# The last 32 tokens' gate of a hybrid decoder step: computed in four column groups, its embedding product in another bank, its x and p loaded ahead of time

## What is computed

```python
    x = x + mixed @ w_out
    xn2 = _rmsnorm(x, norm_ffn_g)
    x = x + _peer(xn2.reshape(B * L, D_MODEL), peer_wq, peer_keys, peer_u, peer_v).reshape(B, L, D_MODEL)
    gate = jax.nn.sigmoid(_rmsnorm(x, norm_pl_g) @ w_pl_gate)
    x = x + gate * (p @ w_pl)
    ...
    y_sample = _rmsnorm(hs, final_norm_g)
```

## Time and profile before

| | us |
|---|---|
| median of 3 runs | 3205.69 (3203.79 to 3205.81) |
| the profiled execution | 3209.12 |
| its span in the trace | 3207.1 |
| mean granted TensorE clock | 0.856 of 2.4 GHz |
| PE busy | 2387.9 (74%) |
| DVE busy | 2238.4 (70%) |
| POOL busy | 1325.4 (41%) |
| ACT busy | 951.4 (30%) |

### The profile page before, as it was taken

One profiled execution on the slowest core, in us unless ns is written; L12 is line 12 of the kernel. 1 busy time (PEld: TensorE's weight loads), 2 busy tenths in 40 slices (PEclk: granted clock), 3 DMA queues, 4 the chain that ended last, 5 costly groups with the idle time before them and its releaser, 6 DMA issues.

```text
span 3207.1 us, 53243 instructions
## 1 busy us (share of the span) xinstructions
PE 2387.9 (74%) x20836; PEld 951.4 (30%) x20836; DVE 2238.4 (70%) x5463; ACT 951.4 (30%) x2428; POOL 1325.4 (41%) x1143
## 2 busy tenths in 40 slices
PE   8879999567877778757876767576678676767666
PEld 3643333223333333213432222122222221212112
DVE  1366667768878788756667667587777777777764
ACT  2212232325335344212322222132323232232222
POOL 0024444324334344435565544344444444444441
PEclk9989999888888889867788878788888887888877
DMA  6579999999999999999999999999999999999994
GB/s 262 184 289 421 421 412 419 417 417 390 418 392 406 416 417 416 413 409 418 417 415 412 416 417 394 418 411 420 408 414 407 420 419 421 404 419 407 421 420 183
DMA packets 202995, 1266.96 MB, mean 395 GB/s; under 512 B 24144, under 2 KB 27496, under 8 KB 61040
## 3 DMA queue, kind: packets, MB, share of 16 engines
q0 software_dynamic: 159808, 1133.76, 86.1%
q1 hardware_dynamic: 41500, 129.51, 10.2%
q10 hardware_dynamic: 1436, 0.29, 0.0%
HBM read 1235.00 MB, written 28.65 MB: 394 GB/s over the span
## 4 chain that ended last, share of the span: by engine, by line
DMA 30%; PE 15%; DVE 6%; POOL 3%; issue 3%; ACT 2%; DVEq 2%; POOLq 0%; ACTq 0%
DMA ring<-in_uv,idx 30%; PE sc L964 7%; DVE ring L1793 3%; PE sc L997 3%; POOL ring L1975 3%; PE route L939 1%; DVEq L1803 1%; PE sc L966 1%; ACT diag L1334 1%; PE work L985 0%; POOL front L1991 0%; ACT hgelu L1329 0%; PE sc L863 0%; PE sc L661 0%; PE sc L957 0%
## 5 line engine op out<-in xcount | busy, mean ns | idle before, releaser
L1975 POOL DMA_INDIRECT ring<-in_uv,idx x1056 | 1246.9, 1181 | 1655.0 <-PE sc L966 1417.6
L1793 DVE CUSTOM_DVE_ANT_0 ring<-ring,xn_cur 128x1024 f32<-128x1024 f32 x1056 | 1280.6, 1222 | 651.0 <-DMA ring<-in_uv,idx 646.4
L964 PE MATMUL sc<-ring,diag 32*32 32x512 f32 x8192 | 1240.8, 725 | 656.2 <-ACT diag L1334 607.9
L966 PE MATMUL sc<-ring,diag 32*32 32x512 f32 x8192 | 1240.9, 725 | 0.0
L964 PEld LDWEIGHTS sc<-ring,diag 32*32 32x32 f32 x8192 | 271.3, 118 | 1437.9 <-ACT diag L1334 1037.1
L1329 ACT ACTIVATE hgelu<-hdot 128x2 f32<-128x2 f32 x528 | 107.5, 204 | 1821.5 <-DVE hdot L1793 1820.5
L1334 ACT ACTIVATE diag<-gate_d,hgelu 128x32 f32<-128x32 f32 x1056 | 281.8, 314 | 21.2
L966 PEld LDWEIGHTS sc<-ring,diag 32*32 32x32 f32 x8192 | 270.6, 118 | 2.3 <-issue 2.3
L521 PE MATMUL sc<-big,front 128*128 128x512 f32 x448 | 209.0, 611 | 4.6 <-DVE front L1439 4.6
L1329 ACT ACT_TABLE_LOAD x128 | 164.2, 1283 | 2.3
L939 PE MATMUL route<-big,xnT 128*128 128x256 f32 x560 | 138.8, 403 | 0.0
(11 more groups left out here) (271 smaller groups left out, 2340.8 us busy)
## 6 DMA issues: line engine op xcount, KB each, us to landing
front<-wqk_scratch SPq DMA_DIRECT2D x27, 1024.0 KB, 13.1
ring<-in_uv,idx POOLq DMA_INDIRECT x1056
big<-in_w_in SPq DMA_DIRECT2D x8, 1024.0 KB, 14.4
wqk_scratch<-front SPq DMA_DIRECT2D x8, 1024.0 KB, 6.6
big<-wqk_scratch SPq DMA_DIRECT2D x8, 1024.0 KB, 22.5
x<-x_scratch SPq DMA_DIRECT2D x13, 512.0 KB, 8.8
front<-in_x SPq DMA_DIRECT2D x8, 512.0 KB, 8.1
xnT<-in_wq_t POOLq DMA_DIRECT2D x8, 512.0 KB, 4.8
```

The lines of the kernel that those rows point to most:

```text
L964: pe.matmul(sc[own, 0, :], diag[own, r, :], uv_rows[own, r, D:D + W4], start=opens_sum, stop=closes).then_inc(row_added[r], 1)
L966: pe.matmul(sc[other, 1, :], diag[own, r, :], uv_rows[own, r, D + W4:2 * D], start=opens_sum, stop=closes).then_inc(row_added[r], 1)
L1793: dve.tensor_tensor_reduce(uv_rows[:, k % RING, 0:D], uv_rows[:, k % RING, 0:D], xn_cur[:, :], 1.0, 0.0, ALU.mult, ALU.add, hdot[:, n % 2, ...
L1975: pool.indirect_dma_start(uv_rows[:, k % RING, :], None, uv, bass.IndirectOffsetOnAxis(ap=idx[:, n % PH, j:j + 1], axis=0)).then_inc(row_i ...
```

## The change

Jobs 0 to 7, the prompt tiles, stay as they are, except that tile 8 leaves `GATE_JOBS`. Tile 8's gate gets functions of its own:

- **x.** SP loads the 32 rows into `xn_next` (`x2_s`) at s = 514, as soon as DVE has copied `xn_next` for tile 8, and no longer into `x2` after tile 7's y is stored.
- **p.** SP loads it at s = 525, after PE's last embedding matmul of tile 7, and no longer after tile 7's y.
- **Embedding.** PE computes it right behind the last `add_rows`, before it waits for x, for all 1024 columns at once: column group q (partitions 32q to 32q+31 of bank RT) holds columns 256q to 256q+255.
- **Gate.** x is turned in 32-row blocks (8 transposes to 128 x 32 in one bank), scaled by one DVE instruction, and multiplied by w_gate in four column groups in bank S0, 32 matmuls of 256 columns.
- **Sigmoid.** One activation of 128 x 256, with the norm factor copied to all four groups by three small DVE copies.
- **The end.** Four DVE products of 32 x 256 bring the groups back to 32 x 1024; then one addition, squares, root, reciprocal, scaling and the store, on 32 partitions.

```diff
-GATE_JOBS = [(4, 322), (0, 342), (3, 361), (5, 384), (1, 404), (6, 448), (2, 468), (7, 512), (8, NN * PAIRS)]
+GATE_JOBS = [(4, 322), (0, 342), (3, 361), (5, 384), (1, 404), (6, 448), (2, 468), (7, 512)]
...
+        x2_s = xn_next[0:NS, :]
+        junk_s = xn_cur[0:NS, :]
+        prod_s = xnT[0:NS, :, :].rearrange("p a b -> p (a b)")
+        x2T_s = cut(fr, 8192, KD, NS)
+        sig_s = cut(fr, 8448, D // QUADS)
...
+            def sample_gate():
+
+                pe.wait_ge(p_in, 16 * (NT + 1))
+                pe.wait_ge(free[RT], opens(RT, "sample embed", QUADS))
+                for k in range(2):
+                    for q in range(QUADS):
+                        mm = pe.matmul(bank[RT][group[q], 0:D // QUADS], p_sb[:, k, 0:NS], wpl[:, k, quarter[q]],
+                                       start=(k == 0), stop=(k == 1))
+                        if k == 1:
+                            mm.then_inc(ready[RT], 1)
+                pe.wait_ge(x2_ready, 2 * (NT + 1))
+                pe.wait_ge(free[TA], opens(TA, "sample x2"))
+                for k in range(KD):
+                    mm = pe.transpose(bank[TA][:, k * NS:(k + 1) * NS], x2_s[:, k * T:(k + 1) * T], ident[0:NS, 0:NS])
+                mm.then_inc(ready[TA], 1)
+                pe.wait_ge(free[S0], opens(S0, "sample gate", QUADS))
+                pe.wait_ge(free[TA], emptied(TA, "sample x2"))
+                for k in range(KD):
+                    for q in range(QUADS):
+                        mm = pe.matmul(bank[S0][group[q], 0:D // QUADS], x2T_s[:, k, :], wg_sb[:, k, quarter[q]],
+                                       start=(k == 0), stop=(k == KD - 1))
+                        if k == KD - 1:
+                            mm.then_inc(ready[S0], 1)
...
-            for step in range(13):
-                gate_step(len(GATE_JOBS) - 1, step)
+            sample_gate()
...
+            act.wait_ge(x2_sq, NT + 1)
+            act.activation(gst[0:NS, RT2:RT2 + 1], gst[0:NS, NS2:NS2 + 1], ACT.Sqrt).then_inc(x2_root, 1)
+            act.wait_ge(r2_ready, NT + 1)
+            act.wait_ge(ready[S0], filled(S0, "sample gate"))
+            act.activation(sig_s, bank[S0][:, 0:D // QUADS], ACT.Sigmoid, scale=gst[:, R2:R2 + 1]).then_inc(free[S0], 1)
+            act.wait_ge(y_sq, NT + 1)
+            act.activation(gst[0:NS, RT3:RT3 + 1], gst[0:NS, NS3:NS3 + 1], ACT.Sqrt).then_inc(y_root, 1)
...
+            def sample_gate():
+
+                dve.wait_ge(x2_s_in, 16)
+                for r in range(RING):
+                    dve.wait_ge(row_added[r], added(NN * TOPK))
+                dve.tensor_tensor(x2_s[:, 0:W4], x2_s[:, 0:W4], sc[0:NS, 0, :], ALU.add).then_inc(x2_ready, 1)
+                dve.tensor_tensor(x2_s[:, W4:D], x2_s[:, W4:D], sc[NS:2 * NS, 1, :], ALU.add).then_inc(x2_ready, 1)
+                dve.drain()
+                dve.tensor_tensor_reduce(junk_s, x2_s, x2_s, 1.0, 0.0, ALU.mult, ALU.add, gst[0:NS, NS2:NS2 + 1])
...
+                for q in range(QUADS):
+                    ins = dve.tensor_tensor(prod_s[:, quarter[q]], sig_s[group[q], :], bank[RT][group[q], 0:D // QUADS],
+                                            ALU.mult)
+                ins.then_inc(free[RT], 1)
+                dve.drain()
+                dve.tensor_tensor(x2_s, x2_s, prod_s, ALU.add)
...
-                if t == NT:
-                    sp.dma_start(y_s, x2[0:NS, :]).then_inc(y_out, 16)
+                sp.dma_start(y_p[tile_rows(t), :], x2[:, :]).then_inc(y_out, 16)
+                if t == NT - 1:
                     return
...
+                if s == N0 * PAIRS + 2:
+                    sp.wait_ge(xn_moved, NT + 1)
+                    sp.dma_start(x2_s, x1_d[SEQ:SEQ + NS, :]).then_inc(x2_s_in, 16)
+                if s == GATE_JOBS[-1][1] + 13:
+                    sp.wait_ge(ready[WK], filled(WK, ("embed", len(GATE_JOBS) - 1, 1)))
+                    load_p(NT)
```

More of the change, by code:

```diff
@@ L341, in front_and_experts @@
         g_pl = cut(fr, 12544, KD)
+        x2_s = xn_next[0:NS, :]
[3 more added lines that the diff above has]
+        sig_s = cut(fr, 8448, D // QUADS)
+        group = [slice(q * NS, (q + 1) * NS) for q in range(QUADS)]
+        quarter = [slice(q * D // QUADS, (q + 1) * D // QUADS) for q in range(QUADS)]
         sc = whole.enter_context(nc.psum_tensor("sc", [T, 4, 512], f32))
@@ L435, in front_and_experts @@
         x2_in = sem("x2_in")
+        x2_s_in = sem("x2_s_in")
         p_in = sem("p_in")
@@ L1836, in add_sum @@
                 dve.wait_ge(x2_in, 16 * X2_LOADS[t])
-                end = NN if t == NT else (t + 1) * PH
                 for r in range(RING):
[L1839 to L1843, removed]
+                    dve.wait_ge(row_added[r], added((t + 1) * PH * TOPK))
+                dve.tensor_tensor(x2[:, 0:W4], x2[:, 0:W4], sc[:, 0, :], ALU.add).then_inc(x2_ready, 1)
+                for m in range(QUADS):
                     own, other = slice(m * NS, (m + 1) * NS), slice((m ^ 1) * NS, ((m ^ 1) + 1) * NS)
@@ L1887, in gate_step @@
                                              in1=g_fin, op0=ALU.mult, op1=ALU.mult).then_inc(y_ready, 1)
+            def sample_gate():
[6 more added lines that the diff above has]
+                dve.tensor_tensor_reduce(junk_s, x2_s, x2_s, 1.0, 0.0, ALU.mult, ALU.add, gst[0:NS, NS2:NS2 + 1])
+                mean_eps(gst[0:NS, NS2:NS2 + 1], D).then_inc(x2_sq, 1)
+                dve.wait_ge(ready[TA], filled(TA, "sample x2"))
+                dve.tensor_tensor(x2T_s, bank[TA][:, 0:KD * NS].rearrange("p (a b) -> p a b", a=KD),
+                                  g_pl.unsqueeze(2).to_broadcast([T, KD, NS]), ALU.mult).then_inc(free[TA], 1)
+                dve.wait_ge(x2_root, NT + 1)
+                dve.reciprocal(gst[0:NS, R2:R2 + 1], gst[0:NS, RT2:RT2 + 1])
+                dve.drain()
+                for q in range(1, QUADS):
+                    dve.tensor_copy(gst[group[q], R2:R2 + 1], gst[0:NS, R2:R2 + 1])
+                dve.drain()
+                dve.sem_inc(r2_ready, 1)
+                dve.wait_ge(free[S0], emptied(S0, "sample gate"))
+                dve.wait_ge(ready[RT], filled(RT, "sample embed"))
+                for q in range(QUADS):
+                    ins = dve.tensor_tensor(prod_s[:, quarter[q]], sig_s[group[q], :], bank[RT][group[q], 0:D // QUADS],
+                                            ALU.mult)
+                ins.then_inc(free[RT], 1)
+                dve.drain()
+                dve.tensor_tensor(x2_s, x2_s, prod_s, ALU.add)
+                dve.drain()
+                dve.tensor_tensor_reduce(junk_s, x2_s, x2_s, 1.0, 0.0, ALU.mult, ALU.add, gst[0:NS, NS3:NS3 + 1])
+                mean_eps(gst[0:NS, NS3:NS3 + 1], D).then_inc(y_sq, 1)
+                dve.wait_ge(y_root, NT + 1)
+                dve.reciprocal(gst[0:NS, R3:R3 + 1], gst[0:NS, RT3:RT3 + 1])
+                dve.drain()
+                dve.scalar_tensor_tensor(out=x2_s, in0=x2_s, scalar=gst[0:NS, R3:R3 + 1], in1=g_fin[0:NS, :],
+                                         op0=ALU.mult, op1=ALU.mult).then_inc(y_ready, 1)
@@ L1944, in _ @@
                         gate_step(i, s - s0)
-            add_sum(NT)
-            for step in range(16):
-                gate_step(len(GATE_JOBS) - 1, step)
+            sample_gate()
         @block.gpsimd
@@ L2245, in step @@
                 for i, (t, s0) in enumerate(GATE_JOBS):
-                    if t < NT and s == s0 + 16:
+                    if s == s0 + 16:
                         after_gate(i)
+                if s == N0 * PAIRS + 2:
[4 more added lines that the diff above has]
+                    load_p(NT)
             load_x(0)
@@ L2268, in _ @@
                 step(s)
-            after_gate(len(GATE_JOBS) - 1)
+            sp.wait_ge(y_ready, NT + 1)
+            sp.dma_start(y_s, x2_s).then_inc(y_out, 16)
             sp.wait_ge(y_out, 16 * (NT + 1))
```

3 lines of the change are left out of this document (removed).

## The result

The changed kernel takes 3188.09 us (median of 5 runs, 3185.96 to 3192.11), the kernel before beside it 3205.81 (5 runs, 3203.79 to 3207.86): ratio 0.9941, 95% interval 0.9930 to 0.9951. On another chip, later, it took 3186.26 (4 runs) against 3207.24, ratio 0.9938 (0.9922 to 0.9953). The forecast was 3185.0 with a range of 3180 to 3191: faster, as forecast, and inside the range; 17.7 us of the 20.7 forecast show in the medians. The profiled execution of the changed kernel, 3185.96 us with a span of 3184.0, is the fastest of its five, and that of before was 3.4 us above its median, so the 23.1 us between the spans flatter the change. What can be compared is the tail: from the end of PE's last row sum to the end of the span. It was 39.2 us and is 19.6. The other 3.5 of the 23.1 lie before it, where the loop has hardly been changed.

The account below looks back on a forecast made before the run. Bound: the serial chain at the end, after the expert fetches. Savings of 3.3 us from x, about 14.8 to the gate's end and 3.2 after, less 0.6 for loads, give 20.7: 3205.69 - 20.7 = 3185.0 us, range 3180 to 3191.

Parts of the forecast that it names:

- The bound of x: Before tile 8's first addition: loading x early gives 3.3 us and no more, up to PE's last row sum.
- Embedding and transposes: On PE between row sums and gate: hidden beside DVE's sum and squares, counted as nothing; worst end costs 0.4 us.
- The gate's matmuls: Tile 8's gate on PE: 64 records in four column groups, 3.66 us at 2.4 GHz instead of 13.75.
- The gate's clock: PE at tile 8's gate: full clock assumed; rising inside or after the gate adds 0 to 3.4 us.
- the rival: PE's clock stays at 1.2 GHz into or through the gate: 1.5 to 3.4 us more, chance 0.25.
- the second case: Clock low for part or all of tile 8's gate, transposes not counting as activity: 3186.5 to 3188.8 us, chance 0.25.
- the first (3183.5 to 3186.5): Whole forecast as worked out, with full clock at tile 8's gate: 3183.5 to 3186.5 us, chance 0.52.
- The table load on the path: ACT between gate and sigmoid: the 1.28 us table load stays on the path; hidden, 1.3 us less, chance 0.07.
- From the gate's end to the end: Sigmoid, products, addition and the unchanged rest of tile 8: 10.7 us; about 3.2 us of the saving.
- The sum of the tail: From last row sum to span's end: 3.3 us saved by x, about 14.8 to the gate's end, 3.2 after.
- The two loads: Early x and p loads beside the expert fetches: cost 0.6 us by bytes; hurting the fetches more, chance 0.09.
- My sign for this: Last expert fetch lands within 1 us of 3162.4; 3 or more later, the loads or something unseen in the loop cost it.

Follow-up runs that it names:

- x_only: Kernel before, with only tile 8's x and p loaded ahead; 3202.84 us against 3207.79, ratio 0.9981.
- late_x: Changed kernel with tile 8's x loaded only after tile 7's y is stored; 3190.28 us, ratio 0.9940 to the kernel before.
- embed_last: Changed kernel with the embedding's eight matmuls moved behind the gate's on PE; 3187.16 us, ratio 0.9932 to the kernel before.
- one_group: Changed kernel without column groups, gate and embedding 512 columns wide in two banks each; 3199.54 us, ratio 0.9977 to the kernel before.
- after_again: Changed kernel profiled once more, unedited; tail 19.66 us, gate 5.12 us.
- table: Changed kernel plus a one-column sigmoid behind ACT's root, loading the sigmoid's table under the gate; 3183.49 us, ratio 0.9920 to the kernel before.
- best: Changed kernel with turned x scaled before the squares and the sigmoid's table loaded under the gate; 3183.86 us, ratio 0.9933 to the kernel before.
- one_product: As best, but one 128 x 256 product and four additions replace four products and one addition; 3185.28 us, ratio 0.9933 to the kernel before.
- turn_first: Changed kernel with DVE scaling the turned x before taking the squares; 3186.45 us, ratio 0.9935 to the kernel before.
- bridge: Changed kernel plus three unread matmuls on PE between transposes and gate; 3188.03 us, ratio 0.9936 to the kernel before; repeated once, 3185.42 us.

## Why the prediction was right, and where not

**The bound of x.** Right: 3.3 us forecast for x ahead; 3.2 measured in x_only, and 2.2 of wait given back in late_x with its smaller load. The row sums, not the store and load of 6 us, set it, as the earlier trace rows had said. The handover is 0.17 us, not 0.05; DVE's addition stands behind waits for all eight slots, which may be the reason, but no run tests it.

**Embedding and transposes.** Right that they cost nothing: the transposes ended at 3166.74, and DVE took them at 3167.60, when the squares were done. That the embedding's place in front is not worth anything either (embed_last) was not said.

**The gate's matmuls.** The form was right, 3.66 us at 2.4 GHz against 13.9, by the row of the same form. The four groups are side by side (one_group). The estimate of 4.3 us from the share for three groups on the Trainium skill's page "TensorE: Matmul & The Clock Gate" (Part 3: Packing small matmuls) is not what the trace shows: 13.92 / 3.66 = 3.8 times.

**The gate's clock** is the step that failed, a mis-sized term: I took full clock (0.52, against 0.25 for a low one), for 3.66 us, and it was 5.04 in the profile. Two premises stood under it, and both were wrong.

The first was that PE would be busy over 5 us in one piece, from the row sums through the embedding to 3169.5 or later, with one pause before the gate. In the changed kernel's profile it was busy from 3162.53 to 3165.30, 2.8 us: the row sums ran at 2.4 GHz and took 1.9 us instead of 3.6. Where they ran at the low clock, as in after_again, it was 4.5 us. And the embedding ends before the second addition does, so that there are two pauses, 0.75 us before the transposes and 1.44 before the gate.

The second was that 2.5 us without a matmul had left the clock at 1.00. That row ends at 3154.3, where work began again. The row after it says 0.50, and the trace of before shows the fall between them, with PE busy:

```profile
3154.40:3155.10 0.70, 0.70 (x4) 0.25 (x6) 0.66 (x1) 0.15 (x1) 0.00 (x0) 1.00 0.96 398
3155.20:3156.20 1.00, 1.00 (x4) 0.18 (x2) 0.95 (x1) 0.00 (x0) 0.00 (x0) 0.50 0.96 401
```

The stretch at 0.50 from 3145.0 had begun in the same way, 0.5 us after work had come back from a pause of 3.06 us. So the row that was read as speaking for the full clock spoke for the rival: a fall can come after the work has come back.

What the runs showed in its place: of the eight profiles of column-grouped gates without filling (late_x, changed, after_again, embed_last, table, best, one_product, turn_first) seven had 5.0 to 5.6 us; turn_first alone had 3.66. With filling it was 3.66 three times of three, and one_group, with 3.4 us of embedding in front, had 1.00 from the start. That little work before the gate lowers its clock, and that filling helps, is thus well supported, above all by the two pairs under bridge. Why turn_first escaped is open: its row sums ran at the low clock, so that its embedding took longest (1.41 us for the last 12 records) and its gate also began early; no run takes these two apart.

The rule that spoke for the second case, that transposes do not count as PE's activity (the Trainium skill, "TensorE: Matmul & The Clock Gate", Part 4: PE-mode transpose), was not tested by itself: embed_last, with only transposes between row sums and gate, had the gate of 5.09 us that the changed kernel has.

By its time my second case (3186.5 to 3188.8) can be neither confirmed nor ruled out. The median of 3188.09 lies in it, and that of the same kernel on the other chip, 3186.26, in the first (3183.5 to 3186.5). The range is 11 us wide and this term missed by 1.4, so that the time fell inside it says nothing for this step.

**The table load on the path.** Right: it began at 3173.40, after the gate's end, and table took that 1.3 us away.

**From the gate's end to the end.** 10.7 us forecast, 10.79 measured. The four products took 1.70 (1.75 forecast), the addition 1.21 (1.23), the sigmoid 0.47 (0.46).

**The sum of the tail.** Forecast 39.2 - 21.3 = 17.9, measured 19.6: 1.4 of the 1.6 us missing are the gate's clock, the rest handovers. The steps of the gain, by kernels that each add one part: x and p ahead 39.2 to 35.35; narrow job with early embedding to 28.97 (no run divides this step, of which 3.7 us are the late embedding); column groups to 19.56.

**The two loads.** 0.6 us forecast for their share of the fetches; it is 1.1 to 1.35. What shows it is the stretch from DVE's copy for tile 8 to the landing of the last fetch, which ends before the last row sums, whose clock differs from profile to profile. It was 78.84 us before (3083.53 to 3162.37), 79.24 in late_x, where p comes ahead but not x, and 79.93 to 80.19 in all twelve profiles with both loads ahead. So p cost about 0.4 us and x about 0.8, more than the bytes gave and far from the upper end of 5.5. It rests on one execution of before and one of late_x. DVE's copy in the timeline of before:

```profile
3083.53 0.69 DVE L1831 COPY xn_cur<-xn_next 128x1024 f32<-128x1024 f32 x1
```

And in that of the changed kernel, whose last fetch landed at 3145.29 + 15.35 = 3160.64, 80.09 us later:

```profile
3080.55 0.69 DVE L1869 COPY xn_cur<-xn_next 128x1024 f32<-128x1024 f32 x1
```

My sign for this, a landing within 1 us of 3162.4 on the same axis, could not have told it, for the same two lines show the other thing that the sum did not contain. Up to this copy nothing in the loop has been changed, and it comes at 3077.0 to 3085.5 in the fourteen profiles. The loop's end moves by some 8 us from one execution to another, more than any single term here but the gate. Of the 23.1 us between the two spans, 19.6 are the tail and 3.0 this copy's earlier place. The 17.7 us of the medians, and the 21.0 of the other chip, so near the 20.7 forecast, are within this scatter; that 21.0 agrees is luck. Put together from the pieces, the gain is 19.6 - 1.2 = 18.4 us, which agrees with the ratio 0.9941, 18.9 us: 20.7 less the 1.6 of clock and handovers and the 0.6 by which the loads cost more.

## What to carry to other kernels

Where a chain at the end has no loop beside it, cost it row by row from rows of the very same form, and compare the tails of profiles rather than total times: effects of 1 us could be read there while the runs scattered by 6, except that the gate's clock differed between executions. A load taken off the path is worth only the distance to the next thing that is late. When a PE stage is made four times shorter, ask what its clock will be: when you look for it in a trace, look also behind the end of a pause, since the fall can come after the work is back. Cheap matmuls into a free bank in the pauses ahead of it gave back 1.4 us, and a table load that stands behind the wait for PE gives back 1.3 for one small activation.

## What the runs showed of the hardware that was not expected

The granted clock fell to 0.50 around the start of a stage that followed 1.5 us of work in 3.6, though no single idle piece was over 1.44 us. Where it fell differs: in the changed kernel at 3167.6, 0.6 us before the gate, and in best and one_product 0.2 and 0.7 us after the gate had begun. In the kernel before it fell at 3155.1, with PE busy again for 0.7 us after a pause of 2.6. Narrowing the pauses alone did not help in two of three profiles (best and one_product with 0.75 and 0.61 us: 5.35 us of gate; turn_first with 0.42 and 0.61: 3.66); filling them with matmuls of 128 x 128 weights did in three of three.
